# First quarter of the weights on ScalarE's DMA queue, and 26 products of zeros ahead of the first true product, in a two-block transformer kernel

## The chip, the cores and the metric

The kernel runs on one core of one Trainium2 chip. The metric is the device time of one execution in microseconds (us), the median of several runs. Beside it there is one profiled execution, from which all rows below are taken.

## What is computed

Two blocks in sequence on 256 tokens of width 1024, everything in float32 precision. The first block has an mLSTM layer, a window attention layer and a SwiGLU after each of them; the second has two attentions side by side (one over a compressed latent, one with a forget gate) that are gated, mixed and normalised. Only its first step matters for the change: the RMS norm of the input and the projection of the normalised input to queries, keys, values and gates.

```python
def rmsnorm(x, w):
    y = xf * lax.rsqrt(jnp.mean(xf * xf, axis=-1, keepdims=True) + EPS)
    return (y * w.astype(jnp.float32)).astype(x.dtype)

def mlstm_mixer(h, w_in, b_gate, norm_w, w_out):
    proj = h @ w_in                      # (256 x 1024) @ (1024 x 3088)
    q = proj[..., :o1] ...               # o1 = 512: the first 512 columns
```

## The kernel before

All weights are cut on the host into chunks of 1024 x 512 (`w_main`), and each chunk into eight tiles of 128 rows. A chunk comes in two halves of four tiles, 1 MB each, into `w_raw`. To keep float32 precision with the fast matmul format, ScalarE rounds each tile to `w_hi` and VectorE forms the remainder `w_lo = w_raw - w_hi`; the activations are split in the same way into `x_hi` and `x_lo`. TensorE then makes three products for each pair (`mm3`, lines 452 to 454): hi by hi, lo by hi, hi by lo. So each byte of weight goes through a chain: transfer by SyncE's queue, ScalarE, VectorE, TensorE. The next half is asked for by SyncE when VectorE is done with the old one (`main`, line 342, which waits on `w_lo_ok`). Narrower weights come as units of 128 x 1024 (`w_side`, `s_raw`, `s_hi`, `s_lo`).

The start of the program is its own case. There is nothing to work on yet, so the first chunk (`C_MQ`, the queries) and the transposed input `xt` are handled tile by tile, k = 0 to 7:

- SyncE issues, in this order: `xt` tiles 0 and 1 (line 353), the parameters `par` with the norm's weights (354), weight tiles 0 and 1, which is the first quarter of the chunk (356, semaphore `w_first`), `xt` tiles 2 to 7 (357), weight tiles 2 and 3 (358), weight tiles 4 to 7 (342), the two row halves of the input `h` (361), the identity (362), the first side unit (363).
- ScalarE rounds `xt` tile k (line 1278) and then weight tile k (line 1283), for k = 0 to 7, with two sums of squares of `h` (line 1289) put in after k = 5 and k = 6. Then come the side unit (1215) and the halves of chunk 1 (1269).
- VectorE follows with the two remainders of each k (lines 1810 and 1813), then the side unit (1722), the first half of chunk 1 (1803), the steps of the inverse root, a copy `r0_row` (1823) that needs a transpose by TensorE (line 595), and the second half of chunk 1 (1803).
- TensorE makes for each k twelve products of 256 columns: two halves of `halves_tile`, each of two blocks by three products. Then come 24 products with the side unit (the gates), 24 with the first half of chunk 1, and so on.

GpSimd sets constants at the start (lines 401 to 406) and issues a transfer of its own (407). At this time `g_hi` is unused apart from its first 512 columns, and `bank[7]` is a free accumulator.

Of the kernel before, what the change touches and what calls it, by code (L numbers as in the profile page):

```python
# [26 lines left out]
P = 128  # L27
# [137 lines left out]
def two_blocks(nc, w_main, w_side, params, rows, c_l0, c_l1, c_b2, ident_d, x_d, x_t, meta_d, pos_d, out_d):  # L165
    ctx = ExitStack()
    with ctx:
# [133 lines left out]
            sem("in_landed"), sem("meta_landed"), sem("c0_landed"), sem("c1_landed"), sem("c2_landed"))  # L301
        pos_landed, rowg_landed = sem("pos_landed"), [sem("rowg_landed0"), sem("rowg_landed1")]
        silu_ok, g_tp, g_hi_ok, g_lo_ok = sem("silu_ok"), sem("g_tp"), sem("g_hi_ok"), sem("g_lo_ok")
        one_ok = sem("one_ok")
        out_landed = sem("out_landed")

        def landed(i):
# [29 lines left out]
        @block.sync  # L337
        def _(sp):
            def main_half(c, g):

                dst = w_raw[:, g, :, :].rearrange("p k n -> p (k n)")
                sp.dma_start(dst, w_main[c, g]).then_inc(w_landed[g], 16)

            def main(c):
                for g in range(2):
                    sp.wait_ge(w_lo_ok, 2 * c - 1 + g)
                    main_half(c, g)

            def side(u, slot):
                sp.wait_ge(s_lo_ok, u - 1)  # L350
                sp.dma_start(s_raw[:, slot, :], w_side[u]).then_inc(s_landed[slot], 16)

            sp.dma_start(xt[:, 0:2, :].rearrange("p k t -> p (k t)"), x_t[:, 0:2 * S]).then_inc(xt_landed[0], 16)
            sp.dma_start(par[:, :], params).then_inc(par_landed, 16)
            first = w_raw[:, 0, :, :].rearrange("p k n -> p (k n)")
            sp.dma_start(first[:, 0:2 * CH], w_main[0, 0][:, 0:2 * CH]).then_inc(w_first, 16)
            sp.dma_start(xt[:, 2:KT, :].rearrange("p k t -> p (k t)"), x_t[:, 2 * S:]).then_inc(xt_landed[1], 16)
            sp.dma_start(first[:, 2 * CH:], w_main[0, 0][:, 2 * CH:]).then_inc(w_landed[0], 16)
            main_half(0, 1)
            for r in range(R):  # L360
                sp.dma_start(h[:, r, :], x_d[r * P:(r + 1) * P, :]).then_inc(x_landed[r], 16)
            sp.dma_start(ident[:, :], ident_d).then_inc(in_landed, 16)
            sp.dma_start(s_raw[:, 0, :], w_side[0]).then_inc(s_landed[0], 16)
            main(1)
            sp.dma_start(s_raw[:, 1, :], w_side[1]).then_inc(s_landed[1], 16)
            main(2)
            side(2, 0)
            with sp.Fori(3, C_FFN[0] + 2) as c:
                main(c)

            def ffn(layer):

                c0, u0 = C_FFN[layer] + 2, U_DOWN[layer] + 2
                with sp.Fori(0, FB - 1) as i:
                    main(c0 + i)
                    for s in range(2):
                        side(u0 + 2 * i + s, (u0 + s) % 2)

            ffn(0)
            main(C_AKV + 1)  # L380
            for u in (U_DOWN[1], U_DOWN[1] + 1):
                side(u, u % 2)
            with sp.Fori(C_AKV + 2, C_FFN[1] + 2) as c:
                main(c)
            ffn(1)
            for c, units in ((C_FK, (U_K, U_V)), (C_FK + 1, (U_Q, U_Q + 1)), (C_FQ, (U_Q + 2,)), (C_FQ + 1, (U_Q + 3,))):
                main(c)
                for u in units:
                    side(u, u % 2)
            with sp.Fori(C_FV, N_CHUNKS) as c:  # L390
                main(c)
            out_rows = out_d.rearrange("(r p) d -> p r d", p=P)
            for i, (r, part) in enumerate(OUT_PARTS):
                sp.wait_ge(z_ok, Z_GATED + i + 1)
                sp.dma_start(out_rows[:, r, part], XN[:, r, part]).then_inc(out_landed, 16)
            sp.wait_ge(out_landed, 16 * len(OUT_PARTS))


        @block.gpsimd
        def _(pool):  # L400
            pool.memset(stat[:, :], 1.0).then_inc(one_ok, 1)
            pool.memset(row_1[0:H0, :, :], 1.0)
            pool.memset(n_hl[0:36, :].bitcast(F32), 0.0)
            pool.memset(i_hl[0:36, :].bitcast(F32), 0.0)
            pool.memset(v_aug[:, :, :, DV:DV + 1], 1.0)
            pool.memset(v_aug[:, :, :, DV + 1:VW], 0.0).then_inc(va_ok, 1)
            pool.dma_start(l0c[:, 0:2 * P], c_l0[:, 0:2 * P]).then_inc(c0_landed, 16)

            pool.wait_ge(mc_ok, 1)
            pool.wait_ge(kn_ok, 2)  # L410
            for hh in range(H0):
                for d in range(2):

                    if hh:
                        pool.wait_ge(c_ps, 2 * hh + d - 1)
                    a = 32 + d * H0 + hh
                    pool.tensor_scalar(m_kw[:, d, :], m_kn[:, d, hh, :], mcol[:, a:a + 1], None, ALU.mult).then_inc(kw_ok, 1)
                if hh:
                    pool.wait_ge(n_ps, 4 * hh)
                pool.wait_ge(ei_ok, hh + 1)  # L420
                for d in range(2):
                    ins = pool.tensor_tensor(m_qi[:, d, :], mqT[:, hh, (1 - d) * P:(2 - d) * P], m_ei[:, d, :], ALU.mult)
                ins.then_inc(qi_ok, 1)
                if hh == H0 - 1:

                    pool.wait_ge(w_hi_ok, 2 * (C_MO + 2) + 2)
                    pool.wait_ge(w_lo_ok, 2 * (C_MO + 2) + 1)
                    pool.tensor_tensor(w_lo[:, 0, 4:8, :], w_raw[:, 1, :, :], w_hi[:, 0, 4:8, :], ALU.subtract).then_inc(w_lo_ok, 1)

                n = USE[("mo", hh // 2, hh % 2)]  # L430
                pool.wait_ge(acc_free[n % 2], n // 2 + 1)
                og = o_gate[:, hh % 2, hh // 2 * CH:(hh // 2 + 1) * CH]
                pool.tensor_scalar(og, og, 1.0, None, ALU.add).then_inc(og1_ok, 1)

            pool.wait_ge(h_ready, 1)
            pool.dma_start(hm[0:M, :], meta_d).then_inc(meta_landed, 16)
            pool.dma_start(a_mask, c_l1.rearrange("p (r s) -> p r s", r=R)).then_inc(c1_landed, 16)
            pool.dma_start(pos_i[:, :], pos_d.to_broadcast([P, S])).then_inc(pos_landed, 16)

            pool.wait_ge(h_ready, 3)  # L440
            pool.dma_start(b2c, c_b2[:, 0:L + S]).then_inc(c2_landed, 16)
            pool.dma_start(b2k, c_b2[:, L + S:]).then_inc(c2_landed, 16)
            pool.dma_start(row_g, rows[0]).then_inc(rowg_landed[0], 16)
            pool.wait_ge(og_ok, 4)
            pool.dma_start(row_g, rows[1]).then_inc(rowg_landed[1], 16)
# [3 lines left out]
        def _(pe):  # L449
# [109 lines left out]
            def halves_tile(c, key, b0, k, to=None):  # L559
# [13 lines left out]
                    done(ins, key)  # L573
                return ins

            for k in range(KT):
                pe.wait_ge(xt_lo, k + 1)
                for i in range(2):
# [624 lines left out]
        def _(act):  # L1203
# [65 lines left out]
                act.activation(w_hi[:, slot, 4 * g:4 * g + 4, :], w_raw[:, g, :, :], ACT.Copy).then_inc(w_hi_ok, 1)  # L1269


            act.wait_ge(one_ok, 1)
            act.activation(stat[:, 30:31], stat[:, 30:31], ACT.Square)
            act.wait_ge(par_landed, 16)
# [1388 lines left out]
```

## Time and profile before

| what | value |
|---|---|
| median of 3 runs | 973.01 us (971.74 to 973.33) |
| profiled execution | 971.56 us |
| its span, first to last instruction | 969.7 us |
| TensorE busy | 938.5 us, 97% |
| VectorE busy | 584.7 us, 60% |
| ScalarE busy | 478.1 us, 49% |
| read from memory | 148.50 MB |

The profiled execution took 1.86 us more than its span, and 1.45 us less than the median of the runs. Times of rows are counted from the start of the span. In a row of the timeline the first number is the start, the second the duration; rows of one engine can overlap, since matmuls are pipelined: how fast they follow one another is read from their starts.

### The profile page before, as it was taken

The page shows a single profiled execution, that of the slowest core. Times are in us where ns is not written, and L with a number is a line of the kernel's source. Part 1 is how long each engine was busy: PE and PEld are TensorE (multiplying, and loading weights), DVE is VectorE, ACT ScalarE, POOL GpSimd, SP SyncE. Part 2 cuts the span into 40 slices and gives each one's busy share as a digit, 9 for nine tenths or more (in the row PEclk, how much of TensorE's full clock was granted, in tenths as well). Part 3 has the DMA queues.
Part 4 walks back from the last instruction along what each step waited for, and adds up shares of the span by engine and source line. Part 5 has one row for each costly group of instructions (what it writes and reads, how often), then busy time and mean ns, then how long its engine had stood idle before and what let it go on. Part 6 is the DMA issues. An engine that isn't in the chain of part 4 may idle for free.

```text
span 969.7 us, 13666 instructions
## 1 busy us (share of the span) xinstructions
PE 938.5 (97%) x5035; PEld 778.2 (80%) x5035; DVE 584.7 (60%) x1078; ACT 478.1 (49%) x770; POOL 24.7 (3%) x39
## 2 busy tenths in 40 slices
PE   6999899999999999899999999999999999999996
PEld 6877677888888898777888888889987877888775
DVE  5966857545454688456445454877665556565665
ACT  5556566353443548364353444686344455445442
POOL 0013200000000000000000000000000000000000
PEclk9999999999999999999999999999999999999998
DMA  8551345645546322245644546232423242433441
GB/s 296 213 195 66 134 146 217 223 168 179 210 156 234 131 87 89 87 147 199 233 157 167 222 148 240 90 130 89 173 92 126 87 164 98 174 120 131 167 169 44
DMA packets 25607, 150.30 MB, mean 155 GB/s; under 512 B 3024, under 2 KB 3152, under 8 KB 11344
## 3 DMA queue, kind: packets, MB, share of 16 engines
q1 hardware_dynamic: 24912, 147.44, 41.6%
q0 software_dynamic: 640, 2.11, 0.7%
q8 instruction: 36, 0.59, 0.3%
q14 instruction: 19, 0.16, 0.0%
HBM read 148.50 MB, written 1.05 MB: 154 GB/s over the span
## 4 chain that ended last, share of the span: by engine, by line
PE 83%; DVE 8%; ACT 3%; DMA 2%; issue 1%; DVEq 1%; SPq 0%; ACTq 0%
PE bank L452 24%; PE bank L453 24%; PE bank L454 23%; DVE w_lo L1803 2%; DMA w_raw<-w_main_dram 2%; PE bank L523 2%; PE bank L1008 1%; PE bank L732 1%; DVE arena L2191 1%; PE bank L1023 1%; PE bank L1061 1%; PE bank L1043 1%; PE bank L1044 1%; DVE w_lo L1782 1%; PE bank L845 1%
## 5 line engine op out<-in xcount | busy, mean ns | idle before, releaser
L452 PE MATMUL bank<-w_hi,x_hi 128*128 128x512 f32 (+2 forms) x648 | 262.4, 405 | 1.3 <-DVE w_lo L1717 0.8
L453 PE MATMUL bank<-w_lo,x_hi 128*128 128x512 f32 (+2 forms) x648 | 253.6, 391 | 0.0
L454 PE MATMUL bank<-w_hi,x_lo 128*128 128x512 f32 (+2 forms) x648 | 252.2, 389 | 0.0
L1717 DVE TENSOR_TENSOR w_lo<-w_raw,w_hi 128x2048 fp32r<-128x2048 f32 x50 | 114.6, 2292 | 106.3 <-ACT w_hi L1208 105.5
L1208 ACT ACTIVATE w_hi<-w_raw 128x2048 fp32r<-128x2048 f32 x54 | 103.4, 1917 | 105.9 <-DMA w_raw<-w_main_dram 102.2
L452 PEld LDWEIGHTS bank<-w_hi,x_hi 128*128 128x128 f32 x648 | 122.2, 189 | 32.1 <-issue 5.6
L454 PEld LDWEIGHTS bank<-w_hi,x_lo 128*128 128x128 f32 x648 | 121.7, 188 | 27.3
L453 PEld LDWEIGHTS bank<-w_lo,x_hi 128*128 128x128 f32 x648 | 122.0, 188 | 22.4
L1803 DVE TENSOR_TENSOR w_lo<-w_raw,w_hi 128x2048 fp32r<-128x2048 f32 x51 | 116.2, 2284 | 6.2 <-ACT w_hi L1269 6.1
L1269 ACT ACTIVATE w_hi<-w_raw 128x2048 fp32r<-128x2048 f32 x50 | 94.9, 1908 | 14.8 <-DMA w_raw<-w_main_dram 14.2
L452 PE MATMUL bank<-x_hi,w_hi 128*128 128x256 f32 (+1 forms) x272 | 79.7, 293 | 9.2 <-DVE w_lo L1813 8.9
L454 PE MATMUL bank<-x_hi,w_lo 128*128 128x256 f32 (+1 forms) x272 | 77.1, 284 | 0.0
L453 PE MATMUL bank<-x_lo,w_hi 128*128 128x256 f32 (+1 forms) x272 | 77.1, 284 | 0.0
L1410 ACT ACTIVATE ffn_nat<-bank,stat 128x256 f32<-128x256 f32 x44 | 20.8, 473 | 109.4 <-PE bank L454 109.2
L1486 ACT ACTIVATE arena<-arena,small 128x144 f32<-128x144 f32 x64 | 29.5, 462 | 77.7 <-DVE small L2168 77.7
L452 PE MATMUL bank<-s_hi,g_hi 128*128 128x512 f32 x166 | 65.4, 394 | 0.5 <-ACT arena L1229 0.5
L454 PE MATMUL bank<-s_hi,g_lo 128*128 128x512 f32 x166 | 65.4, 394 | 0.0
L453 PE MATMUL bank<-s_lo,g_hi 128*128 128x512 f32 x166 | 65.3, 393 | 0.0
L452 PEld LDWEIGHTS bank<-x_hi,w_hi 128*128 128x128 f32 x272 | 51.9, 191 | 12.7 <-issue 11.8
L452 PE MATMUL bank<-w_hi,s_hi 128*128 128x512 f32 x128 | 53.1, 415 | 3.9 <-DVE h L1994 2.8
L2063 DVE SCALAR_TENSOR_TENSOR ffn_nat<-bank,stat,ffn_nat 128x256 f32<-128x256 f32 x44 | 21.1, 481 | 58.9 <-ACT ffn_nat L1410 58.8
L453 PEld LDWEIGHTS bank<-x_lo,w_hi 128*128 128x128 f32 x272 | 51.9, 191 | 0.0
(357 smaller groups left out, 1451.8 us busy)
## 6 DMA issues: line engine op xcount, KB each, us to landing
w_raw<-w_main_dram SPq DMA_DIRECT2D x111, 1024.0 KB, 5.4
s_raw<-w_side_dram SPq DMA_DIRECT2D x51, 512.0 KB, 4.2
w_raw<-w_main_dram SPq DMA_DIRECT2D x2, 512.0 KB, 7.1
h<-x_dram SPq DMA_DIRECT2D x2, 512.0 KB, 11.2
arena<-rows_dram POOLq DMA_DIRECT2D x2, 512.0 KB, 4.0
arena<-x_t_dram SPq DMA_DIRECT2D x1, 768.0 KB, 7.8
out_dram<-arena SPq DMA_DIRECT2D x1, 512.0 KB, 2.6
out_dram<-arena SPq DMA_DIRECT2D x2, 256.0 KB, 2.1
```

The lines of the kernel that those rows point to most:

```text
L452: pe.matmul(out, ah, bh, start=first, stop=False)
L453: pe.matmul(out, ah, bl, start=False, stop=False)
L454: return pe.matmul(out, al, bh, start=False, stop=last)
L523: ins = pe.transpose(b[:, M + r * P:M + (r + 1) * P], src(r, k), ident[:, :])
L732: ins = pe.transpose(bank[2][:, ks * S + r * P:ks * S + (r + 1) * P], ffn_nat[:, 1, r, ks * P:(ks + 1) * P], ident[:, :])
L1208: act.activation(w_hi[:, slot, 4 * g:4 * g + 4, :], w_raw[:, g, :, :], ACT.Copy).then_inc(w_hi_ok, 1)
L1269: act.activation(w_hi[:, slot, 4 * g:4 * g + 4, :], w_raw[:, g, :, :], ACT.Copy).then_inc(w_hi_ok, 1)
L1410: act.activation(ffn_nat[:, 0, r, :], acc[(n0 + r) % 2][:, 0:256], ACT.Silu, scale=stat[:, 24 + r:25 + r]).then_inc(silu_ok, 1)
L1486: ins = act.activation(tiles(r), tiles(r), ACT.Exp, bias=small[:, s0 + 2 + r:s0 + 3 + r], accum_out=small[:, s0 + 4 + r:s0 + 5 + r])
L1717: dve.tensor_tensor(w_lo[:, slot, 4 * g:4 * g + 4, :], w_raw[:, g, :, :], w_hi[:, slot, 4 * g:4 * g + 4, :], ALU.subtract).then_inc(w_lo_o ...
L1803: dve.tensor_tensor(w_lo[:, slot, 4 * g:4 * g + 4, :], w_raw[:, g, :, :], w_hi[:, slot, 4 * g:4 * g + 4, :], ALU.subtract).then_inc(w_lo_o ...
L2063: dve.scalar_tensor_tensor(out=ffn_nat[:, 1, r, :], in0=acc[b_][:, 256:512], scalar=root_col(r), in1=ffn_nat[:, 0, r, :], op0=ALU.mult, op ...
```

## The change

Three things are edited. The transfer of weight tiles 0 and 1 goes from SyncE's queue, where it was third, to ScalarE's queue, as the first instruction of that engine's program. GpSimd clears a 128 x 256 piece of `g_hi` as its first instruction of the block. TensorE waits for that and then multiplies this piece with itself 26 times into `bank[7]`, each product with 256 columns, and nobody reads the outcome.

```diff
+        one_ok, idle_ok = sem("one_ok"), sem("idle_ok")
+        idle_r = g_hi[:, 512:512 + 2 * P]
...
             sp.dma_start(xt[:, 0:2, :].rearrange("p k t -> p (k t)"), x_t[:, 0:2 * S]).then_inc(xt_landed[0], 16)
             sp.dma_start(par[:, :], params).then_inc(par_landed, 16)
             first = w_raw[:, 0, :, :].rearrange("p k n -> p (k n)")
-            sp.dma_start(first[:, 0:2 * CH], w_main[0, 0][:, 0:2 * CH]).then_inc(w_first, 16)
             sp.dma_start(xt[:, 2:KT, :].rearrange("p k t -> p (k t)"), x_t[:, 2 * S:]).then_inc(xt_landed[1], 16)
...
         @block.gpsimd
         def _(pool):
+            pool.memset(idle_r.bitcast(F32), 0.0).then_inc(idle_ok, 1)
             pool.memset(stat[:, :], 1.0).then_inc(one_ok, 1)
...
+            pe.wait_ge(idle_ok, 1)
+            for _ in range(26):
+                pe.matmul(bank[7][:, 0:2 * P], idle_r[:, 0:P], idle_r, start=True, stop=True)
             for k in range(KT):
                 pe.wait_ge(xt_lo, k + 1)
...
+            act.dma_start(w_raw[:, 0, 0:2, :].rearrange("p k n -> p (k n)"), w_main[0, 0][:, 0:2 * CH]).then_inc(w_first, 16)
             act.wait_ge(one_ok, 1)
             act.activation(stat[:, 30:31], stat[:, 30:31], ACT.Square)
```

The first instructions of SyncE's program in the kernel before (`arena` is here the transposed input `xt`):

```order
L337 UNCONDITIONAL_BRANCH [waits barrier_Pool_Activation_PE_DVE_SP_release]
L353 DMA arena<-x_t_dram 128x512
L354 DMA par<-params_dram 128x81
L356 DMA w_raw<-w_main_dram 128x1024
L357 DMA arena<-x_t_dram 128x1536
L358 DMA w_raw<-w_main_dram 128x1024
L342 DMA w_raw<-w_main_dram 128x2048
```

And in the changed kernel, where the lines below the edits have other numbers:

```order
L338 UNCONDITIONAL_BRANCH [waits barrier_Pool_Activation_PE_DVE_SP_release]
L354 DMA arena<-x_t_dram 128x512
L355 DMA par<-params_dram 128x81
L357 DMA arena<-x_t_dram 128x1536
L358 DMA w_raw<-w_main_dram 128x1024
L343 DMA w_raw<-w_main_dram 128x2048
```

The rest of the input and all later loads stand one place further up. The first instructions of ScalarE's program in the changed kernel:

```order
L1206 UNCONDITIONAL_BRANCH [waits barrier_Pool_Activation_PE_DVE_SP_release]
L1276 DMA w_raw<-w_main_dram 128x1024
L1278 ACT_TABLE_LOAD
L1278 ACTIVATE stat<-stat 128x1 [waits one_ok]
L1283 ACTIVATE x_hi<-arena,par 128x256 [waits xt_landed0,par_landed]
L1288 ACTIVATE w_hi<-w_raw 128x512 [waits w_first]
```

The load stands ahead of the table load, which was the first instruction before; the order behind it is as it was. The first instructions of TensorE's program in the changed kernel:

```order
L449 UNCONDITIONAL_BRANCH [waits barrier_Pool_Activation_PE_DVE_SP_release]
L579 MATMUL bank<-g_hi 128x256 [waits idle_ok]
L579 MATMUL bank<-g_hi 128x256 x25
L453 MATMUL bank<-x_hi,w_hi 128x256 [waits q_lo_ok,xt_lo]
L454 MATMUL bank<-x_lo,w_hi 128x256
```

Before, the product that waits for `q_lo_ok` and `xt_lo` was the first; the 26 are now ahead of it.

## Rows read from the trace of the kernel before

**Rows 1.** The page: busy time of the engines over the span.
```profile
PE 938.5 (97%) x5035; PEld 778.2 (80%) x5035; DVE 584.7 (60%) x1078; ACT 478.1 (49%) x770; POOL 24.7 (3%) x39
```

**Rows 2.** Waits of TensorE over the whole span: total us, times, longest.
```profile
PE bank L452 <- DVE w_lo L1813: 8.9, 1, 8.9
PE bank L452 <- DVE h L1994: 2.8, 2, 2.4
...
PE bank L452 <- DVE w_lo L1717: 0.8, 1, 0.8
```

**Rows 3.** Timeline, 0 to 9 us: the issues and the path to the first product.
```profile
0.73 1.28 ACT L1273 ACT_TABLE_LOAD   x1 [0.73 <-PEq L2657]
0.74 0.39 SPq L353 DMA_DIRECT2D arena<-x_t_dram  x1
1.19 0.42 SPq L354 DMA_DIRECT2D par<-params_dram  x1
1.66 0.42 SPq L356 DMA_DIRECT2D w_raw<-w_main_dram  x1
1.72 0.30 POOL L404 MEMSET g_lo<- 36x256 f32 x1
2.12 0.43 SPq L357 DMA_DIRECT2D arena<-x_t_dram  x1
4.57 0.51 ACT L1278 ACTIVATE x_hi<-arena,par 128x256 fp32r<-128x256 f32 x1 [2.34 <-DMA par<-params_dram]
7.42 0.63 ACT L1283 ACTIVATE w_hi<-w_raw 128x512 fp32r<-128x512 f32 x1 [2.34 <-DMA w_raw<-w_main_dram]
8.91 0.55 PE L452 MATMUL bank<-x_hi,w_hi 128*128 128x256 f32 x1 [8.91 <-DVE w_lo L1813]
```

**Rows 4.** Timeline of TensorE: products of tiles 0 and 1, start and duration.
```profile
11.19 0.41 PE L453 MATMUL bank<-x_lo,w_hi 128*128 128x256 f32 x1
11.40 0.41 PE L454 MATMUL bank<-x_hi,w_lo 128*128 128x256 f32 x1
11.62 0.39 PE L452 MATMUL bank<-x_hi,w_hi 128*128 128x256 f32 x1
11.83 0.29 PE L453 MATMUL bank<-x_lo,w_hi 128*128 128x256 f32 x1
11.96 0.28 PE L454 MATMUL bank<-x_hi,w_lo 128*128 128x256 f32 x1
12.08 0.28 PE L452 MATMUL bank<-x_hi,w_hi 128*128 128x256 f32 x1
```

**Rows 5.** Timeline, ScalarE and VectorE: what makes tile 2, tile 4 and tile 7 ready.
```profile
9.97 0.51 ACT L1278 ACTIVATE x_hi<-arena,par 128x256 fp32r<-128x256 f32 x1 [1.01 <-DMA arena<-x_t_dram]
11.01 0.63 ACT L1283 ACTIVATE w_hi<-w_raw 128x512 fp32r<-128x512 f32 x1 [0.54 <-DMA w_raw<-w_main_dram]
11.68 0.69 DVE L1813 TENSOR_TENSOR w_lo<-w_raw,w_hi 128x512 fp32r<-128x512 f32 x1 [0.68 <-ACT w_hi L1283]
13.53 0.63 ACT L1283 ACTIVATE w_hi<-w_raw 128x512 fp32r<-128x512 f32 x1 [0.34 <-DMA w_raw<-w_main_dram]
19.05 0.69 DVE L1813 TENSOR_TENSOR w_lo<-w_raw,w_hi 128x512 fp32r<-128x512 f32 x1
```

**Rows 6.** Timeline: the gates, the inverse root and chunk 1, with their first products.
```profile
20.30 1.23 DVE L1722 TENSOR_TENSOR s_lo<-s_raw,s_hi 128x1024 fp32r<-128x1024 f32 x1 [0.56 <-ACT s_hi L1215]
21.64 0.33 PE L452 MATMUL bank<-x_hi,s_hi 128*128 128x256 f32 x1
22.04 2.29 DVE L1803 TENSOR_TENSOR w_lo<-w_raw,w_hi 128x2048 fp32r<-128x2048 f32 x1 [0.51 <-ACT w_hi L1269]
24.50 0.28 PE L452 MATMUL bank<-x_hi,w_hi 128*128 128x256 f32 x1
27.32 0.38 PE L595 MATMUL bank<-ident,stat 128*128 128x128 f32 x2
28.24 2.29 DVE L1803 TENSOR_TENSOR w_lo<-w_raw,w_hi 128x2048 fp32r<-128x2048 f32 x1
30.25 0.28 PE L454 MATMUL bank<-x_hi,w_lo 128*128 128x256 f32 x1
30.59 0.39 PE L452 MATMUL bank<-x_hi,w_hi 128*128 128x256 f32 x1
```

**Rows 7.** Busy time by stretch: PE, PEld, DVE, ACT, POOL, PEclk, DMA share, GB/s.
```profile
1.50:2.25 0.75, 0.00 (x0) 0.00 (x0) 0.00 (x0) 0.71 (x2) 0.75 (x5) 1.00 0.31 93
2.25:3.00 0.75, 0.00 (x0) 0.00 (x0) 0.00 (x0) 0.00 (x0) 0.49 (x1) 1.00 0.95 185
3.00:3.75 0.75, 0.00 (x0) 0.00 (x0) 0.00 (x0) 0.00 (x0) 0.00 (x0) 1.00 1.14 164
3.75:4.50 0.75, 0.00 (x0) 0.00 (x0) 0.00 (x0) 0.00 (x0) 0.00 (x0) 1.00 0.51 138
4.50:5.25 0.75, 0.00 (x0) 0.00 (x0) 0.05 (x1) 0.51 (x1) 0.00 (x0) 1.00 1.17 328
5.25:6.00 0.75, 0.00 (x0) 0.00 (x0) 0.43 (x1) 0.00 (x0) 0.00 (x0) 1.00 0.86 257
...
9.00:12.00 3.00, 3.00 (x15) 3.00 (x16) 1.58 (x4) 1.50 (x4) 0.00 (x0) 1.00 1.00 420
```

**Rows 8.** The end of the span: last product, and the same columns by stretch.
```profile
961.68 0.40 PE L454 MATMUL bank<-w_hi,x_lo 128*128 128x512 f32 x1
...
961.00:964.00 3.00, 1.08 (x5) 0.56 (x3) 1.55 (x6) 0.69 (x2) 0.00 (x0) 1.00 0.43 175
964.00:966.00 2.00, 0.00 (x0) 0.00 (x0) 1.45 (x8) 0.00 (x0) 0.00 (x0) 0.54 0.00 0
966.00:968.00 2.00, 0.00 (x0) 0.00 (x0) 1.22 (x2) 0.00 (x0) 0.00 (x0) 0.50 0.28 104
```

More of the change, by code:

```diff
@@ L303, in two_blocks @@
         silu_ok, g_tp, g_hi_ok, g_lo_ok = sem("silu_ok"), sem("g_tp"), sem("g_hi_ok"), sem("g_lo_ok")
-        one_ok = sem("one_ok")
+        one_ok, idle_ok = sem("one_ok"), sem("idle_ok")
+        idle_r = g_hi[:, 512:512 + 2 * P]
         out_landed = sem("out_landed")
```

## The prediction

> **What bounds the kernel now.** I begin with the busy shares: TensorE has work in 97% of the span, so what moves its end moves the time [rows 1]. Then its waits: one of 8.9 us stands at the very start, the next in size are 2.8 us in two pieces [rows 2]. The change touches that first wait and nothing else, so the question is how much earlier TensorE gets through the start, and whether what it gains there survives. The timeline gives the path to the first product [rows 3]: the weight quarter is issued at 1.66 and landed at 7.42, when ScalarE's wait for it ends; rounding, remainder and the handing on take 1.49 us; the first product starts at 8.91.
>
> The products' starts tell the clock [rows 4]. Up to 11.62 they are 0.21 us apart, from 11.83 on 0.12: 256 columns in 0.21 us is the level of 1.2 GHz, and the step down to 0.12 is the change to 2.4 GHz, somewhat above 256 / 2.4 = 0.107. (The column of the granted clock says 1.00 there [rows 7], but the spacing is plainly halved; I believe the spacing.) From 8.91 to 11.83 there are 13 slow steps, so with 0.095 us too much in each, the cold clock costs TensorE 13 x 0.095 = 1.24 us.
>
> Next I ask for each tile when it was ready and when TensorE came to it. It needs 12 products, 12 x 0.1175 = 1.41 us, for each k. The gates' first product is at 21.64 [rows 6]; going back from it in steps of 1.41, TensorE began k = 7 at 20.23 and k = 2 at 13.18. Ready they were when VectorE's remainder ended: k = 2 at 11.68 + 0.69 = 12.37, k = 7 at 19.05 + 0.69 = 19.74 [rows 5], the gates at 20.30 + 1.23 = 21.53, chunk 1 at 22.04 + 2.29 = 24.33 against a first product at 24.50, its second half at 28.24 + 2.29 = 30.53 against 30.59, ahead of which TensorE even stood for 0.22 us (the product at 30.25 should be followed at 30.37) [rows 6]. So TensorE's lead over its supply shrinks from 0.81 us at k = 2 to 0.49, 0.11, 0.17 and nothing. **From 21 us on the kernel is bound by the chain of transfer, ScalarE and VectorE, not by TensorE's own work**, and at 37 us TensorE waits once more for that chain, 0.8 us [rows 2]. What reaches the end is the shift of this chain, plus at most 0.1 us.
>
> **The change, part by part.**
> 1. *The products of zeros.* GpSimd clears 256 columns ahead of its other work: 0.30 us by the row of another 256 columns [rows 3]. It delays its constants by as much; the earliest use is ScalarE's dummy activation behind the table load, and ScalarE then waits for parameters anyway until 4.57, so it costs nothing. TensorE starts at about 1.1 us. 26 products take 26 x 0.2125 = 5.5 us if all are slow, and 13 x 0.2125 + 13 x 0.1175 = 4.3 us if the clock rises after as many as before. They end at 5.4 to 6.6 us, at least 1.3 us before the first true product can start. So they delay nothing. What they can bring is the 1.24 us of the cold clock.
> 2. *The quarter on ScalarE's queue.* Its issue goes from 1.66 to about 0.73, 0.93 us earlier. ScalarE's table load slips by one issue, about 0.4 us, from 0.73 to 1.15, and ends at 2.4, hidden below the wait until 4.57. If the landing moves with the issue, tile 0 is there at 6.49 and the first product starts at 8.91 - 0.93 = 7.98.
> 3. *SyncE's queue.* Everything behind the removed issue is issued 2.12 - 1.66 = 0.46 us earlier [rows 3]: the rest of the input, weight tiles 2 and 3, 4 to 7, `h`, the side unit.
>
> Now the supply behind the first quarter. ScalarE waits for transfers at k = 2 (9.97 and 11.01) and k = 4 (13.53), and from 13.53 to 22 us it runs without a wait worth naming [rows 5]. So the chain shifts by what the transfer of tiles 4 to 7 shifts. The bounds: the engines move what they move, so below it is zero (or less, see the rivals). Above: from 2.25 to 6.00 us five rows of 185, 164, 138, 328 and 257 GB/s have a mean of 214, against 420 later [rows 7]; if all of it went at 420, 3.75 x (1 - 214/420) = 1.84 us would be won. The shares of the DMA engines say that most of that time is not idle: 0.49, 0.14 and 0.05 of a slice of 0.75 us are unused, together 0.51 us. I take the issue's 0.46, which is nearest to these 0.51: the holes in the stream look like a queue that waits for the next issue.
>
> With 0.46: k = 2 is ready at 11.91, k = 7 at 19.28. TensorE, if warm, has done tiles 0 and 1 at 7.98 + 24 x 0.1175 = 10.80, and then waits 1.1 us. If its clock fell back, it needs the same 13.18 - 8.91 = 4.27 us as before and is there at 12.25, at k = 7 at 19.30 against 19.28. **Warm or cold, it meets the same supply by k = 7; the products of zeros are then worth about nothing.** The sum: 0 for the zeros, 0.93 at the first product of which 0.46 stays, so -0.46 us. Against the profiled execution this is 971.56 - 0.46 = 971.10; that execution lies 1.45 below the median, so against the median it is 973.01 - 0.46 = 972.55, and I say 972.5. A measurement of this kernel tells 0.2%, or 1.95 us, from no change (its three runs lie 1.6 us apart).
>
> **The rivals.**
> - *The transfers gain nothing (973.0).* The DMA engines are shared by all queues, and from 2.25 to 5.25 us their shares are 0.95, 1.14, 0.51 and 1.17, a mean of 0.94: nearly full [rows 7]. If the work is the same and only its order changes, tiles 4 to 7 land when they did, the first product is earlier, and TensorE waits longer at k = 2; gain at most 0.1 us. Against it speaks the slice with 0.51. The Trainium skill has this as a rule (DMA: Bandwidth & Descriptors, "Issuing engines are not separate DMA queues"): transfers issued from different engines run on the same 16 DMA engines and interleave, and a second issuer saves only the time of issuing. By that rule the sum would be between 973.0 and the 0.46 us of one issue; the trace so far agrees with either.
> - *Both parts count (971.2).* The slow start of the transfers is a latency that two queues overlap, and the stream goes at its later rate: the supply shifts by up to 1.84 us. TensorE could follow by 0.93 + 1.24 = 2.17, so here the warm clock is needed. 973.01 - 1.84 = 971.2. For it speaks the low rate of the first slices; against it that the engines are busy at that low rate.
> - *The quarter gets in the way (974.7).* Its 512 KB now travel beside the first input and the parameters, while the stream is at its slowest. If they moved at the 138 GB/s of that stretch, they would take 3.8 us instead of 1.6 at the 328 that the next slice shows, and all behind them is 2.2 us later, less 0.46: +1.7. The point from which it decides: as soon as tiles 4 to 7 land more than 0.1 us later than 13.53, TensorE has no lead left to hide it. Against it: nothing but the order of the packets changes, and the bytes up to tile 7 are the same.
> - *The clock falls again before the true products.* At the end of the span the last product ends at 962.08, and the granted clock is at 0.54 from 964 to 966 and 0.50 after it [rows 8]: some 2 us of rest were enough there, and here are 1.4 to 2.6 us of rest between 5.4 or 6.6 and 7.98. So the zeros may fail at what they are for. By the sum above that costs nothing beside the forecast, except in the second rival, where it would take back up to 1.24 us.
>
> **How the numbers follow.** Forecast (chain shifts by 0.3 to 0.9) 0.57; no gain from the transfers 0.25; both parts count 0.11; in the way 0.07. The range goes from 971.0, where the second rival and a low run lie, to 973.9, which is the first rival's 973.0 with the scatter of the runs on top; the forecast's own is 972.0 to 972.8. Faster than 0.2% needs 971.06 or less: a large part of the case at 971.2, and a little of the scatter, 0.12. Slower than 0.2% needs 974.96: 0.04. The rest is 0.84.
>
> **What would show it.** Right: 26 rows before 7 us, the first at about 1.1; the issue of the quarter at 0.73 and ScalarE's first wait for weights ended near 6.5; a first true product near 8.0; a new wait of about 1 us ahead of k = 2; the gates' first product near 21.2, and every later row shifted by the same 0.4 to 0.5 us. The spacing of the first true products tells whether the clock was kept. Wrong: tiles 4 to 7 rounded at 13.5 or later (first or third rival), or before 12.5 (second), and the gates' first product earlier by over 1 us. Should the span be shorter by more than the shift at 31 us, then something later that I take for rigid was not.

## The result and the profile after

The changed kernel is slower, by 0.15% or 1.89 us. The forecast was 972.5 us, about 0.5 us faster, which is less than these runs can tell. Of the executions reported below, one (of the kernel with 56 zeros alone) took 1880.89 us, about twice the usual time, and is left out of the ratios.

| | before | after |
|---|---|---|
| median | 972.99 us (971.74 to 973.84, 20 runs) | 974.88 us (972.26 to 976.38, 20 runs) |
| ratio, 95% interval | | 1.0015 (1.0008 to 1.0022) |
| profiled execution | 971.56 us | 975.02 us |
| its span | 969.7 us | 973.2 us |

The timeline of the changed kernel up to its first true product (start, duration, engine, line):

```profile
0.73 0.41 ACTq L1276 DMA_DIRECT2D w_raw<-w_main_dram  x1
0.74 0.39 SPq L354 DMA_DIRECT2D arena<-x_t_dram  x1
1.09 4.92 PE L579 MATMUL bank<-g_hi 128*128 128x256 f32 x26 [1.09 <-POOL g_hi L401]
1.19 0.42 SPq L355 DMA_DIRECT2D par<-params_dram  x1
7.12 0.51 ACT L1283 ACTIVATE x_hi<-arena,par 128x256 fp32r<-128x256 f32 x1 [4.45 <-DMA par<-params_dram]
7.54 0.61 ACT L1288 ACTIVATE w_hi<-w_raw 128x512 fp32r<-128x512 f32 x1
9.03 0.55 PE L453 MATMUL bank<-x_hi,w_hi 128*128 128x256 f32 x1 [3.01 <-DVE w_lo L1818]
```

The issue moved as forecast, and the 26 zeros ran from 1.09 to 6.01. But the parameters, which landed at 4.57 before [rows 3], now land at 7.12. The weight quarter is there when ScalarE comes to it at 7.54. The first true product is at 9.03, not at 7.98: later than before.

Its clock, by stretches (columns as in [rows 7]):

```profile
6.00:8.00 2.00, 0.01 (x1) 0.00 (x0) 0.25 (x1) 0.88 (x2) 0.00 (x0) 1.00 1.02 415
8.00:9.00 1.00, 0.00 (x0) 0.01 (x1) 1.00 (x3) 1.00 (x3) 0.00 (x0) 0.51 1.05 430
9.00:11.00 2.00, 1.98 (x9) 2.00 (x10) 1.36 (x3) 0.98 (x3) 0.00 (x0) 0.50 1.03 430
11.00:13.00 2.00, 2.00 (x11) 2.00 (x10) 1.69 (x3) 1.67 (x4) 0.00 (x0) 0.50 0.99 406
13.00:15.00 2.00, 2.00 (x11) 2.00 (x11) 1.73 (x4) 1.91 (x4) 0.00 (x0) 0.54 1.04 406
15.00:17.00 2.00, 2.00 (x20) 2.00 (x19) 1.29 (x3) 2.00 (x5) 0.00 (x0) 1.00 1.08 446
```

The granted clock falls at about 8 us, some 2 us after the last product of zeros, and is back only between 14 and 15. The spacing of the products shows the same step:

```profile
14.50 0.41 PE L454 MATMUL bank<-x_lo,w_hi 128*128 128x256 f32 x1
14.71 0.35 PE L455 MATMUL bank<-x_hi,w_lo 128*128 128x256 f32 x1
14.89 0.28 PE L453 MATMUL bank<-x_hi,w_hi 128*128 128x256 f32 x1
15.01 0.28 PE L454 MATMUL bank<-x_lo,w_hi 128*128 128x256 f32 x1
```

From 9.03 to 14.71 there are 26 steps at the slow spacing, against 13 before, and the next is 0.18 us. What that does further on, first in the kernel before and then in the changed one (the copy `r0_row`, the issue of a weight half, ScalarE's rounding when it has landed):

```profile
27.74 0.42 DVE L1823 COPY arena<-bank 128x256 f32<-128x256 f32 x1 [0.63 <-PE bank L595]
30.56 0.33 SPq L342 DMA_DIRECT2D w_raw<-w_main_dram  x1
35.27 1.92 ACT L1208 ACTIVATE w_hi<-w_raw 128x2048 fp32r<-128x2048 f32 x1 [3.71 <-DMA w_raw<-w_main_dram]
```

```profile
29.07 0.42 DVE L1828 COPY arena<-bank 128x256 f32<-128x256 f32 x1 [2.41 <-PE bank L599]
31.89 0.33 SPq L343 DMA_DIRECT2D w_raw<-w_main_dram  x1
38.06 1.92 ACT L1212 ACTIVATE w_hi<-w_raw 128x2048 fp32r<-128x2048 f32 x1 [7.16 <-DMA w_raw<-w_main_dram]
```

The copy is 1.33 us later: 13 more slow steps at 0.095 us each are 1.24, and the half-slow one and a first product that is 0.11 later are about as much as the rest. The copy waits 2.41 us for TensorE's transpose, not 0.63, so TensorE and no longer the supply binds there. Then the weight half takes 38.06 - 31.89 = 6.17 us from issue to use, against 4.71, which adds another 1.46. At 37 us of the old time VectorE is 2.79 us behind; by 62 us it has won back some and is 1.99 behind (the same instructions of VectorE compared in both timelines). At 400 us it is still 1.9.

And a third place, near 410 us, behind the rest of 2.4 us that both kernels have there ([rows 2] has its size). The first line of the stretches is of the kernel before, whose clock is full there in this profile; the others are of the changed kernel:

```profile
410.50 0.57 PE L453 MATMUL bank<-w_hi,s_hi 128*128 128x512 f32 x1 [2.39 <-DVE h L1999]
```

```profile
410.00:412.00 2.00, 2.00 (x11) 1.65 (x10) 1.75 (x1) 0.09 (x1) 0.00 (x0) 1.00 0.62 262
```

```profile
410.00:412.00 2.00, 1.50 (x4) 1.23 (x5) 1.69 (x3) 1.33 (x1) 0.00 (x0) 0.70 0.87 262
412.00:414.00 2.00, 2.00 (x6) 1.52 (x6) 1.65 (x1) 0.07 (x1) 0.00 (x0) 0.50 0.62 262
```

There the shift goes from 1.9 to 3.5 us, which is the whole difference of the two spans. Comparing these two profiles overstates what the change does: 3.5 us, where the medians differ by 1.89.

The mean granted clock is known for every execution. It is 0.997 in the first profile of before, 0.995 in a second one (below), which has one fall of the clock near 410 us, and 0.993 in this profile of the changed kernel. Of the changed kernel's 20 executions 11 have 0.992 or 0.993, and their median is 975.1 us; the six with 0.995 have 973.6, the one with 0.997 took 972.41. Of 95 executions of the kernel before, timed beside the experiments, 55 have 0.997, 38 have 0.995 or 0.996, and none is below 0.994. So the longer time at half clock is not a matter of this one profile.

### The profile page after: what moved, and what is told of

It reads as the page before. It is cut to its first block, busy times and chain, and to the rows that moved or that the text cites. A ratio compares the mean times of both kernels' runs of the same rounds, so it can differ in the third digit from the quotient of the medians.

```text
span 973.2 us, 13719 instructions
## 1 busy us (share of the span) xinstructions
PE 946.5 (97%) x5061; PEld 785.3 (81%) x5061; DVE 585.9 (60%) x1078; ACT 480.2 (49%) x770; POOL 25.0 (3%) x40
## 3 DMA queue, kind: packets, MB, share of 16 engines
HBM read 148.50 MB, written 1.05 MB: 154 GB/s over the span
## 4 chain that ended last, share of the span: by engine, by line
PE 84%; DVE 8%; ACT 3%; DVEq 1%; issue 1%; DMA 1%; SPq 0%; ACTq 0%
PE bank L453 25%; PE bank L454 24%; PE bank L455 24%; DVE w_lo L1808 2%; PE bank L524 2%; PE bank L1012 1%; PE bank L736 1%; DVE arena L2196 1%; PE bank L1027 1%; PE bank L1065 1%; PE bank L1048 1%; PE bank L1047 1%; DVE w_lo L1787 1%; DMA w_raw<-w_main_dram 1%; PE bank L849 1%
## 5 line engine op out<-in xcount | busy, mean ns | idle before, releaser
L2068 DVE SCALAR_TENSOR_TENSOR ffn_nat<-bank,stat,ffn_nat 128x256 f32<-128x256 f32 x44 | 21.2, 483 | 97.6 <-ACT ffn_nat L1415 97.2
```

What stands on the lines that cost most here:

```text
L2068: dve.scalar_tensor_tensor(out=ffn_nat[:, 1, r, :], in0=acc[b_][:, 256:512], scalar=root_col(r), in1=ffn_nat[:, 0, r, :], op0=ALU.mult, op ...
```

## The experiments

In all of them "before" is the kernel before, timed on the same chip beside each group: 973.02, 973.16 and 973.14 us in the three groups. A median is of 11 or 12 runs unless said.

### One part alone: the zeros, the moved quarter, more zeros, the parameters first

Theory A: the loss is the clock, which rises early, falls in the rest and comes back late. Theory B: the loss is the moved transfer, which delays the parameters.

**The 26 zeros alone**, the quarter back in third place on SyncE's queue:

```diff
-            act.dma_start(w_raw[:, 0, 0:2, :].rearrange("p k n -> p (k n)"), w_main[0, 0][:, 0:2 * CH]).then_inc(w_first, 16)
+            sp.dma_start(first[:, 0:2 * CH], w_main[0, 0][:, 0:2 * CH]).then_inc(w_first, 16)
```

> The 26 products of zeros alone; the first weight quarter is back in third place on SyncE's queue. Theory A (the early products shift where the granted clock changes: it rises early, falls in the rest before the true products, and comes back late): this kernel loses too. The zeros end near 6.0, the first true product is at 8.9 as before, the clock falls near 8 and the true products run 0.21 us apart for over 20 of them, not 13; the copy r0_row starts 1 to 1.5 us later than 27.74; the time is 974.3 to 976 with a spread of several us. Theory B (the loss comes from the moved transfer, which holds up the parameters to 7.1 us): time and trace as before, 973.0, since tile 0 is not later.

Measured: 974.31 (971.78 to 975.29), ratio 1.0010 (1.0001 to 1.0020). The zeros alone lose, by little more than the noise, so B isn't the whole. But the profile doesn't show what A said: the clock does fall at 8.15, but it is back at 11.56, the first true product is at 8.62, 13 steps are slow as before, and the copy is at 27.37. The loss shows later: the weight half issued at 30.19 is used at 36.38, and the clock is at half for a stretch near 115 and one near 411.

**The quarter alone**, the three lines of zeros on TensorE taken out of the changed kernel:

> The quarter on ScalarE's queue alone, no product of zeros. Theory A: parameters land near 7.1, the first true product is at 9.0, the clock is cold for some 13 products from there (as before), the supply chain of k = 2 to 7 is 0.44 us earlier, and the time is 972.5 to 973.1 (gain 0 to 0.45). Theory B: 974.5 to 975, as in the changed kernel.

Measured: 973.53 (972.47 to 974.19), ratio 1.0006 (0.9997 to 1.0015): no difference that this can tell. The parameters land at 7.13 and the first product is at 9.03, exactly as in the changed kernel; 25 steps are slow. This cold stretch is nearly as long as the changed kernel's 26, without any zeros.

**56 zeros alone** (`range(26)` to `range(56)`, the quarter on SyncE's queue):

> As the first of this group, but 56 products of zeros, so that they last until about 9.2 us and the true products follow without rest. Theory A: the clock stays full, all true products are 0.12 us apart, TensorE waits at k = 2 for its supply (12.37), the copy r0_row starts at 27.7 as before, and the time is 972.8 to 973.1, with no gain since the supply binds. Rival (any early product costs, by power or by where the clock's changes fall later on): 974.5 or more although the start is warm. Theory B: 973.0.

Measured: 973.03 (970.40 to 974.51, and the one execution of 1880.89, without which the median is 972.98), ratio 1.0000 (0.9991 to 1.0009). No true product is slow, and the median gains nothing. That rules out that early products as such cost more than 0.9 us. It doesn't show that a warm start is worth nothing: in this profile VectorE is ahead of the first profile of before by 0.6 us at 62 us and at 400, until the clock falls near 408.

**The parameters too on ScalarE's queue, ahead of the quarter:**

```diff
-            sp.dma_start(par[:, :], params).then_inc(par_landed, 16)
...
+            act.dma_start(par[:, :], params).then_inc(par_landed, 16)
             act.dma_start(w_raw[:, 0, 0:2, :].rearrange("p k n -> p (k n)"), w_main[0, 0][:, 0:2 * CH]).then_inc(w_first, 16)
```

> The changed kernel with the parameters also moved to ScalarE's queue, ahead of the weight quarter; SyncE's queue then holds only the input and the later loads. If two queues share the engines packet by packet, the parameters (40 KB) now go out beside the first input and land at 3.5 to 5 us instead of 7.1; the first product then waits for the quarter and starts at 8.0 to 8.9. Supply of k = 2 to 7 earlier by 0.5 to 0.9 us than before the change. With 26 zeros ending at 6.0 the rest is then 2.0 to 2.9 us. Theory A: the time falls only if the clock survives that rest; I expect it mostly falls, 973.5 to 975. Rival (the loss came from the late first product alone, which made the rest too long): 972.5 or less.

Measured: 975.97 (973.63 to 976.98), ratio 1.0024 (1.0014 to 1.0034), the slowest of all. Its timeline:

```profile
5.46 0.51 ACT L1283 ACTIVATE x_hi<-arena,par 128x256 fp32r<-128x256 f32 x1 [2.30 <-DMA par<-params_dram]
9.02 0.63 ACT L1288 ACTIVATE w_hi<-w_raw 128x512 fp32r<-128x512 f32 x1 [3.06 <-DMA w_raw<-w_main_dram]
10.53 0.55 PE L452 MATMUL bank<-x_hi,w_hi 128*128 128x256 f32 x1 [4.32 <-DVE w_lo L1818]
```

The parameters come earlier than in the changed kernel, later than before; the quarter now lands at 9.02, though it is issued at 1.17, and at 1.66 before. Here and in the changed kernel a transfer that stands second in one of two filled queues comes late. The rest behind the zeros grows to 4.3 us, and the time with it.

### The kernel before once more, the rest filled, the parameters ahead of the input, and a filler near 408 us

**The kernel before, unchanged**, for a second profile:

> The kernel before, unchanged, for a second profile: how far do its own start and its clock vary? In the kernels run so far without a moved transfer, tile 2 was ready 0.4 and 0.9 us earlier than in the first profile of before. If that is scatter between executions, this profile shows k = 2 and k = 7 ready somewhere within 1 us of the first. If the granted clock also falls for 3.4 us near 410 us here, as in all four experiments and in the changed kernel but not in the first profile of before, then that fall is a matter of chance and not of the change.

One execution, 973.43. Three of its rows:

```profile
10.70 0.63 ACT L1283 ACTIVATE w_hi<-w_raw 128x512 fp32r<-128x512 f32 x1 [0.76 <-DMA w_raw<-w_main_dram]
13.18 0.63 ACT L1283 ACTIVATE w_hi<-w_raw 128x512 fp32r<-128x512 f32 x1 [0.30 <-DMA w_raw<-w_main_dram]
28.29 0.42 DVE L1823 COPY arena<-bank 128x256 f32<-128x256 f32 x1 [1.54 <-PE bank L595]
```

```profile
410.00:412.00 2.00, 2.00 (x6) 1.63 (x5) 1.93 (x1) 0.00 (x0) 0.00 (x0) 0.50 0.74 311
```

Tile 2 is rounded at 10.70 and tile 4 at 13.18; [rows 5] have 11.01 and 13.53, the changed kernel 10.60 and 13.10. So 0.31 and 0.35 of the "earlier supply" of 0.41 and 0.43 come with no change at all. 23 steps are slow here, not 13, and the copy waits 1.54 us for TensorE: in this execution of the kernel before, TensorE and not the supply binds at the copy. And the clock is at half near 410 us. The first profile had the shorter cold stretch and no such fall; by the mean clocks above, most executions of before have none either.

This second profile divides the loss better than the first, since both it and the changed kernel's have the fall near 410 us. The same instruction of VectorE starts at 63.69 us here and at 65.49 in the changed kernel, 1.80 later; the spans are 971.5 and 973.2, 1.7 apart. Between these two profiles the whole loss is made ahead of 62 us: 0.78 by the copy, and 1.0 behind it.

**The changed kernel with 56 zeros** (`range(26)` to `range(56)`):

> The changed kernel with 56 products of zeros instead of 26: the rest of 3.0 us ahead of the first true product at 9.03 is filled. Theory A (the clock falls in that rest and that is the loss): all true products at 0.12 us, the copy r0_row near 27.3 to 27.7, time 972.6 to 973.2, 1.5 to 2.3 us below the changed kernel. Rival (the late parameters and the two queues are the loss): 974.5 or more.

Measured: 972.73 (970.71 to 973.72), ratio 0.9995 (0.9986 to 1.0004), against 1.0015 with 26. The zeros meet the true products without a rest, and the clock holds:

```profile
1.09 8.84 PE L579 MATMUL bank<-g_hi 128*128 128x256 f32 x56 [1.09 <-POOL g_hi L401]
```

```profile
9.00:11.00 2.00, 2.00 (x19) 2.00 (x19) 1.52 (x4) 0.92 (x3) 0.00 (x0) 1.00 1.08 453
```

The parameters are as late as in the changed kernel (7.28), so their lateness by itself costs nothing that this can tell. Theory B falls. Theory A's number is met; but the added instructions changed something else too, as the last group shows.

**The parameters first on SyncE's queue**, ahead of the input's first tiles, else the changed kernel:

> The changed kernel (26 zeros, quarter on ScalarE's queue) with the parameters issued first on SyncE's queue, ahead of the first input. If the parameters were late only because their packets stood behind the first input's, which took turns with the quarter's, they now land by 4.5 us; the input's first two tiles then land near 6 to 7 as the parameters did, so ScalarE's first rounding starts at 6 to 7 and the first true product at 8.0 to 8.9. The rest behind the zeros is then 2.0 to 2.9 us. Theory A: the clock falls or stays by where its steps lie; the time is between 972.5 and 975, with more runs at the low end than the changed kernel has.

Measured: 973.77 (972.53 to 975.25), ratio 1.0007 (0.9998 to 1.0016). Now the input's tiles, second in the queue, come at 7.15, and the first product is at 9.05. So exchanging these two doesn't help: ScalarE needs both, and the second is late. The zeros take 5.7 us in this profile, the first true products still run fast, and the clock falls at about 10, under them.

**56 zeros, the quarter on SyncE's queue, and a filler near 408 us:**

```diff
+            for _ in range(10):
+                pe.matmul(bank[7][:, :], s_hi[:, 0, 0:P], s_hi[:, 0, 0:512], start=True, stop=True)
             mixer_rest("aout", C_AOUT, "f1", y_hi, y_lo)
```

> As the 56 zeros alone (quarter on SyncE's queue, 973.03), and 10 more products of 512 columns, of data already there, in the rest of 2.4 us near 408 us ahead of line 918, into the free bank 7. Theory A (a rest of 2 us can cost a stretch at half clock, 1.5 us each time): the fall near 410 us is gone, the times at 974 and more become rare, and the median is 0.5 to 1.3 us lower, 971.7 to 972.5. Rival (the filler delays the true products behind it by as much, or the fall only moves elsewhere): 973.0.

Measured: 971.09 (970.50 to 972.88), ratio 0.9982 (0.9973 to 0.9991): faster than both kernels, and below the range I had given. The filler sits in the rest and the clock stays:

```profile
405.62 2.43 PE L924 MATMUL bank<-s_hi 128*128 128x512 f32 x10
```

```profile
410.00:412.00 2.00, 2.00 (x11) 1.64 (x10) 1.33 (x1) 0.46 (x1) 0.00 (x0) 1.00 0.48 197
```

11 products in the stretch, where the half clock allowed 6.

### The count of instructions apart from the work

With ten profiles at hand, one transfer divides them: the weight half issued at about 30 to 33 us. From issue to ScalarE's use it takes 6.05 to 6.24 us in all four kernels with 26 zeros, and 4.67 to 4.82 in the other six. The queues of the transfers differ with it. The kernel before, 30 to 37 us (while the half travels) and 37 to 40:

```profile
q1 hardware_dynamic: 288, 1.57, 59.2%
q14 instruction: 1, 0.01, 0.3%
```

```profile
q1 hardware_dynamic: 56, 0.46, 49.9%
q8 instruction: 1, 0.02, 4.4%
```

The changed kernel, 32 to 37 us, and the changed kernel with 56 zeros, 28 to 30 us, ahead of the issue at 30.33:

```profile
q1 hardware_dynamic: 232, 1.41, 76.4%
q8 instruction: 1, 0.02, 1.4%
```

```profile
q1 hardware_dynamic: 39, 0.19, 22.7%
q8 instruction: 1, 0.02, 2.8%
```

The piece on q8 is a reload of instructions, 16 KB in one packet. With no zeros it starts at 38.1 to 39.4 us, with 26 at 32.4 to 34.7, with 56 at 28.5 to 28.8. Theory C: the number of instructions executed sets when it comes, and 26 more products, 52 instructions with their weight loads, bring it into the transfer on which everything waits.

The trace shows how the transfer ends. These are the last 0.7 us ahead of the landing, first in the kernel before and then in the changed one:

```profile
34.60:35.30 0.70, 0.70 (x9) 0.70 (x8) 0.70 (x2) 0.03 (x1) 0.00 (x0) 1.00 0.86 339
```

```profile
37.40:38.10 0.70, 0.41 (x4) 0.20 (x2) 0.70 (x1) 0.04 (x1) 0.00 (x0) 1.00 0.10 41
```

The DMA engines are busy for 86% of it before, and for 10% in the changed kernel, which is between one and two engines of 16. So nearly all engines have finished, and the half waits for a remainder. The reload's packet took 1.13 us, and the half is 1.46 us late.

**26 products of 8 columns**, nothing else changed in the kernel before:

```diff
+            for _ in range(26):
+                pe.matmul(bank[7][:, 0:8], idle_r[:, 0:P], idle_r[:, 0:8], start=True, stop=True)
```

> The kernel before with 26 early products of only 8 columns each: as many added instructions as in the changed kernel, but hardly any work, and no transfer moved. A new theory C: in all four kernels with 26 zeros the piece of 16 KB on the instruction queue (q8) falls between 32.5 and 34.7 us, inside the transfer of a weight half that is issued at about 30 to 32, and that half lands 6 us after its issue instead of 4.7; with no zeros the piece falls at 38 to 40, with 56 at 28.6 to 29, and the transfer is quick. Theory C expects the piece near 33 again, ScalarE's rounding (line 1208's) that started at 35.27 at 36 or later, and a median of 973.7 to 974.3. If the count of instructions does not matter: 973.1.

Measured: 973.88 (971.80 to 975.33), ratio 1.0006 (0.9997 to 1.0015). The size is as expected, though the interval still reaches no change; the delay of the half is clear in the trace. First the half's issue and use, then q8 from 30 to 37 us:

```profile
30.80 0.33 SPq L343 DMA_DIRECT2D w_raw<-w_main_dram  x1
37.01 1.92 ACT L1213 ACTIVATE w_hi<-w_raw 128x2048 fp32r<-128x2048 f32 x1 [5.57 <-DMA w_raw<-w_main_dram]
```

```profile
q8 instruction: 1, 0.02, 1.5%
```

6.21 us, with no transfer moved and only short products added. The clock rose at about 12.8, in the true products, so these short ones didn't raise it.

**The changed kernel with 30 such short products behind the 26:**

> The changed kernel with 30 products of 8 columns behind the 26 of zeros: the count of the 56 that were good, but the rest ahead of the first true product is still 2 us or more. Theory A alone (the clock's fall is the whole loss): 974.5 to 975.1, as the changed kernel. Theory A and C together: the collision near 34 us is gone, the cold start is not, so 973.5 to 974.1. C alone: 972.7 to 973.2.

Measured: 974.08 (970.69 to 975.20), ratio 1.0012 (1.0003 to 1.0021). The half takes 4.67 us and the reload comes at 28 to 30, as C wants. My premise was wrong: the short ones aren't short. They take 3.41 us for 30, about 0.112 from start to start, and last until 9.1:

```profile
5.71 3.41 PE L581 MATMUL bank<-g_hi 128*128 128x8 f32 x30
```

In this profile, the fastest of all with a span of 968.9, the clock rises at 4.3 and stays. But 9 of the 11 executions have a mean granted clock of 0.992 or 0.995, where this one has 0.997, and they take 973.5 to 975.2 us. So the fall happens in most executions, and the profile caught one of the others. That such short products keep the clock only sometimes is what these numbers suggest; it isn't shown.

**The changed kernel with its 26 zeros 512 columns wide** (`idle_r` is 512 columns of `g_lo`):

> The changed kernel with its 26 zeros 512 columns wide, so that they last until about 8.7 us with the instruction count of the changed kernel. Theory A alone: the clock is full when the true products start, and the time is that of the 56 zeros, 972.6 to 973.1. A and C together: the start is warm but the piece of instructions still meets the weight half near 33 us, so 973.4 to 974.0.

Measured: 973.23 (971.76 to 973.53), ratio 1.0002 (0.9993 to 1.0011). It starts without a rest, the clock is full at the first true product, and the half takes 36.52 - 30.37 = 6.15 us. The value lies between the two ranges that I had written, 0.13 above that of A and 0.17 below that of A and C.

**The kernel before with the 10 filler products near 408 us alone:**

> The kernel before with only the 10 filler products near 408 us (line 918's place), nothing at the start. It separates the two halves of the best version (971.09). If the gain is all from the rest near 408 us: 971.1 to 971.6, a clock without a fall there. If the warm start has a part in it: 971.7 to 972.5.

Measured: 971.70 (970.71 to 973.39), ratio 0.9986 (0.9977 to 0.9995). The value lies on the border of the two cases, and most of the gain of the best version is here: 1.44 us of 2.07. 24 steps were slow at its start, and the copy waits 1.41 us for TensorE. The 0.6 us between the two medians are within the noise; in the profiles VectorE is 1.1 to 1.2 us earlier in the version with the warm start, at 62 us and at 400.

The four kernels with both parts of the change make a table. Each number is the difference to the median of before beside it:

| | reload inside the transfer (26) | reload ahead of it (56) |
|---|---|---|
| rest or short products behind the zeros | +1.89 (the change) | +0.94 (26 and 30 short) |
| no rest | +0.09 (26 wide) | -0.43 (56) |

Down the columns, the rest costs 1.80 and 1.37 us (the second from a kernel whose rest was filled with short products); along the rows, the reload costs 0.95 and 0.52. Each median is known to 0.7 to 0.9 us against before, so the differences down the columns are just beyond the noise, and those along the rows are not.

The profiles give the reload's price more sharply. From 28 to 62 us, a stretch with no fall of the clock in any of them, VectorE loses 0.5 to 0.7 us against the first profile of before in all six kernels with the reload inside the transfer, and gains 0.2 to 0.4 in the other seven profiles. So a part of the 1.4 us is won back by 62 us, and the price that stays is 0.5 to 0.7 us against the first profile and 0.7 to 1.1 against the others. All later reloads come earlier too (the next at 57.7 us against 64.4), but at 400 us the changed kernel is no further behind than at 62.

## Why the prediction was wrong, point by point

- **What bounds the start** held for the one profile that it was read from, and not in general. With 23 and 24 slow steps (the second profile of before, and the kernel with the filler at 408 alone) the copy waits 1.54 and 1.41 us for TensorE. That a warm start is worth little agrees with the medians (56 zeros alone: 973.03 against 973.02) within 0.9 us; but the four profiles with a warm start and the reload out of the way are 0.4 to 0.8 us ahead of even the first profile of before at 62 us.
- **"The products of zeros ... delay nothing. What they can bring is the 1.24 us"** is the step that failed first. I bounded them by their duration, and they do end at 6.01. I didn't count them as instructions. They move the reload of instructions from 38.1 us to 34.7, into the transfer of the weight half issued at 31.89, which takes 1.2 to 1.6 us longer in six profiles of six; of that 0.5 to 1.1 us are left at 62 us. In the sum the zeros stood at 0.
- **"If its clock fell back, it needs the same 4.27 us as before"** is the step that failed next. The fall itself I had seen coming from [rows 8], 2 us after the last product, and it came so. But I took 13 slow products for a fixed cost, from one profile. The profiles without the 256-column zeros have 13, 18, 23, 24 and 25 slow steps, and the changed kernel's has 26. "Warm or cold, it meets the same supply by k = 7" was worked out for 13 slow products from 7.98 on; some ten more would have eaten the 0.93 us of the earlier start. With 26 from 9.03 on there was no such room: the gates' first product came at 23.00 us, where it was 21.64 before and about 21.2 in the forecast, and the copy 1.33 us later. A part of this is scatter of the start, since the kernel before came to the gates at 22.22 in its second profile. I should have asked how many slow steps the forecast could bear.
- **"The issue's 0.46" in the supply** was an artefact that looked like a hit. The changed kernel's tiles came 0.41 and 0.43 us earlier, and the kernel before, run again, came 0.31 and 0.35 earlier. Over all profiles, ScalarE rounds tile 4 at 12.63 to 13.64 us with the quarter on SyncE's queue, and at 12.95 to 13.32 with it on ScalarE's. The first rival, that the transfers gain nothing, was right on this point. The rule of the Trainium skill that it names (DMA: Bandwidth & Descriptors, "Issuing engines are not separate DMA queues") agrees with these traces.
- **The first product at 7.98** was wrong by 1.05 us. I had checked the quarter's way and not that of the parameters beside it, which lost 2.55 us. With 56 zeros, which cover it, it cost nothing (972.73).
- **The rival on the slow side** gave 974.7 and the time is 974.88, but by another mechanism: tiles 4 to 7 were not late. Its number was luck.
- **The range**, 971.0 to 973.9, was built on 1.6 us of scatter in three runs. In 20 runs the changed kernel alone spreads over 4.1 us, and its times go with the mean granted clock: 972.4 at 0.997, 973.6 at 0.995, 975.1 at 0.992 and 0.993.

What stays open: how the 1.89 us of the medians divide between the cold stretch at the start, the reload and later falls of the clock. Against the second profile of before all is lost ahead of 62 us, against the first 1.5 of 3.5 us near 410. In the profile of the zeros alone the start was quick and two later stretches were at half clock. A profile shows one course, and the mean clock of the other executions doesn't say where it was low.

## What to carry to other kernels

Filler products to keep TensorE's clock should reach to the first true product. Here 26 that ended 3 us early cost 1.89 us, and 26 wide ones that reached it cost nothing (+0.09); in the profiled execution of the first the clock came back later (14.85 us) than in any without them (11.8 to 14.5). The rest worth filling was another one, 2.4 us in the middle of the program, where 10 products in a free bank gave 0.14%; look for such rests behind which the product spacing doubles in some profiles. And where a kernel hangs on a single transfer, look at which reload of instructions comes near it before adding instructions anywhere ahead, and take two or three profiles of the kernel before, not one, before a difference of half a microsecond is believed.

## What the runs showed of the hardware

- A reload of instructions, one packet of 16 KB, inside a transfer of 1 MB: 6.05 to 6.24 us from issue to use in six profiles, against 4.67 to 4.82 in eight without it. When the reload comes follows the count of instructions: 38.1 to 39.4 us with none added, 31.4 to 34.7 with 26 products, 28.4 to 28.8 with 56. At the end of the delayed transfer the DMA engines are busy for 10%. That this rest is the work of the engine that carried the reload fits its 1.13 us, but the trace doesn't name the engine.
- The clock fell after 2.0 us of rest (zeros, 6.01 to about 8), and behind the rest of 2.4 us near 408 in 9 of the 12 profiles that have this rest (not in the first one of before, nor in those with 26 short and with 26 and 30 short). It cost 1.4 to 1.6 us each time there.
- The column of the granted clock shows 1.00 from the start until its first change, though the true products run at the slow spacing until then in the kernel before. The spacing is what to trust there, and a cold start is missing from the mean granted clock.
- Products of 8 columns follow one another at 0.21 us cold and 0.112 us warm, those of 256 columns at 0.21 and 0.113 to 0.12, those of 512 at 0.43 and 0.23. So at 8 columns something other than the columns sets the pace, and it happens to be that of 256 columns; what it is, no run shows. My reading of 0.21 us as 256 columns at 1.2 GHz gave the right level, but the spacing alone doesn't prove it.
- Two hardware queues share the DMA engines: from 2 to 4 us of the changed kernel ScalarE's moved 0.21 MB and SyncE's 0.12. With the quarter on ScalarE's queue, the 40 KB of parameters behind 256 KB on SyncE's queue came at 7.12 us instead of 4.57.
